# Low parts of 27 weight tiles made on GpSimd instead of VectorE, and an earlier row plan, in expert pass one of a decoder step

## What is computed

```python
q = jnp.einsum('td,dc->tc', xt, peer_wq).reshape(PEER_BLOCK, PEER_HEADS, 2, D_KEY // 2)
s = jnp.einsum('thcd,hckd->thck', q, peer_subkeys).astype(jnp.float32)
sv, si = lax.top_k(s, PEER_TOPK)
...
expert = i1 * N_KEYS + i2
gate = jax.nn.softmax(cv, axis=-1)
a = jax.nn.gelu(jnp.einsum('td,thkd->thk', xt, expert_u[expert]).astype(jnp.float32))
return jnp.einsum('thk,thkd->td', (gate * a).astype(xt.dtype), expert_v[expert])
```

## Time and profile before

| | |
|---|---|
| time, median of 3 runs | 1692.96 us (1692.66 to 1693.1) |
| profiled execution, its own time | 1686.36 us |
| its span, first to last instruction | 1684.6 us |
| TensorE, TensorE weight load | 98%, 93% busy |
| VectorE, ScalarE, GpSimd | 81%, 43%, 29% busy |
| mean granted TensorE clock | 0.994 of full |
| HBM traffic | 270 GB/s over the span |

### The profile page before, as it was taken

One profiled execution on the slowest core, in us unless ns is written; L12 is line 12 of the kernel. 1 busy time (PEld: TensorE's weight loads), 2 busy tenths in 40 slices (PEclk: granted clock), 3 DMA queues, 4 the chain that ended last, 5 costly groups with the idle time before them and its releaser, 6 DMA issues.

```text
span 1684.6 us, 29339 instructions
## 1 busy us (share of the span) xinstructions
PE 1651.6 (98%) x10256; PEld 1560.4 (93%) x10256; DVE 1368.5 (81%) x2831; ACT 732.8 (43%) x1386; POOL 489.4 (29%) x447
## 2 busy tenths in 40 slices
PE   8998999999999999999999999999999999999999
PEld 6876766679999999999999999999999999999999
DVE  3273456767889999999999989867998999999996
ACT  2121354454214434666666668833333333333332
POOL 0004222200000233322322244342443544454440
PEclk9998999999999999999999999999999999999999
DMA  7617324313225898888988899998999999999994
GB/s 221 196 38 234 92 72 120 95 52 120 75 76 173 272 336 302 285 317 302 329 321 315 312 332 356 358 377 293 355 397 358 375 402 394 399 392 398 400 386 157
DMA packets 187430, 454.16 MB, mean 270 GB/s; under 512 B 25667, under 2 KB 91715, under 8 KB 186819
## 3 DMA queue, kind: packets, MB, share of 16 engines
q1 hardware_dynamic: 110850, 242.39, 41.3%
q0 software_dynamic: 50416, 182.63, 29.5%
q10 hardware_dynamic: 26016, 27.27, 4.7%
HBM read 401.14 MB, written 54.47 MB: 270 GB/s over the span
## 4 chain that ended last, share of the span: by engine, by line
PE 62%; DVE 4%; DMA 3%; issue 1%; SPq 0%; ACT 0%; DVEq 0%; ACTq 0%
PE ps L2060 10%; PE ps L2063 10%; PE ps L2066 10%; PE ps L2036 9%; PE ps L2032 9%; PE ps L2031 9%; PE ps L2082 5%; DMA sb_ring<-expert_v 2%; DMA gates_dense<-sb_g_stage 1%; DVE sb_w_lo L1861 1%; DVE sb_slot L1898 1%; DVE sb_rows_y L1993 0%; DVE sb_hot L1897 0%; DVE sb_hot L1894 0%; DVE sb_xT_sb L2020 0%
## 5 line engine op out<-in xcount | busy, mean ns | idle before, releaser
L1766 ACT ACTIVATE sb_w_hi<-sb_ring 128x1024 fp32r<-128x1024 f32 x254 | 269.4, 1061 | 506.6 <-PE ps L2066 211.7
L1861 DVE TENSOR_TENSOR sb_w_lo<-sb_ring,sb_w_hi 128x1024 fp32r<-128x1024 f32 x255 | 312.4, 1225 | 58.8 <-ACT sb_w_hi L1766 52.4
L2031 PE MATMUL ps<-sb_x_hi,sb_w_hi 128*128 128x384 f32 x1024 | 349.7, 342 | 1.1 <-PEq L1255 1.0
L2032 PE MATMUL ps<-sb_x_lo,sb_w_hi 128*128 128x384 f32 x1024 | 345.2, 337 | 0.0
L2060 PE MATMUL ps<-sb_x_lo,sb_w_hi 128*128 128x384 f32 x1016 | 198.5, 337 | 6.2 <-ACT sb_x_lo L1775 6.1
L2036 PE MATMUL ps<-sb_x_hi,sb_w_lo 128*128 128x384 f32 x1024 | 200.8, 337 | 3.2 <-DVE sb_w_lo L1861 3.2
L2063 PE MATMUL ps<-sb_x_lo,sb_w_lo 128*128 128x384 f32 x1016 | 197.1, 336 | 0.0
L2066 PE MATMUL ps<-sb_x_lo,sb_w_hi 128*128 128x384 f32 x1016 | 196.6, 335 | 0.0
L2031 PEld LDWEIGHTS ps<-sb_x_hi,sb_w_hi 128*128 128x128 f32 x1024 | 192.0, 187 | 1.6 <-issue 1.6
L2032 PEld LDWEIGHTS ps<-sb_x_lo,sb_w_hi 128*128 128x128 f32 x1024 | 192.4, 188 | 0.0
L1756 POOL DMA_INDIRECT sb_scores<-expert_u_rows,sb_row_expert x80 | 101.0, 1263 | 293.5 <-DVE sb_row_dots L1982 206.6
(11 more groups left out here) (338 smaller groups left out, 2502.1 us busy)
## 6 DMA issues: line engine op xcount, KB each, us to landing
sb_ring<-expert_u SPq DMA_DIRECT2D x128, 512.0 KB
sb_ring<-expert_v SPq DMA_DIRECT2D x128, 512.0 KB
gates_dense<-sb_g_stage ACTq DMA_DIRECT2D x12, 2048.0 KB
hid_dense<-sb_hid SPq DMA_DIRECT2D x104, 192.0 KB
sb_scores<-hid_dense SPq DMA_DIRECT2D x104, 192.0 KB
sb_g_stage<-gates_dense SPq DMA_DIRECT2D x32, 384.0 KB
sb_g_stage<-gates_dense SPq DMA_DIRECT2D x48, 256.0 KB
sb_ring<-peer_wq SPq DMA_DIRECT2D x16, 512.0 KB
```

What stands on the lines that cost most here:

```text
L1766: nc.scalar.activation(whi[v % 2][:, :], ring(v)[:, :], ACT.Copy).then_inc(w_hi, 1)
L1861: nc.vector.tensor_tensor(wlo[v % 2][:, :], ring(v)[:, :], whi[v % 2][:, :], ALU.subtract).then_inc(w_lo, 1)
L2031: nc.tensor.matmul(out, hi[:, c * P:(c + 1) * P], g.x_hi[:, c], start=(c == 0), stop=False)
L2032: nc.tensor.matmul(out, hi[:, c * P:(c + 1) * P], g.x_lo[:, c], start=False, stop=False)
```

## The change

GpSimd gets its own `low_part(v)` for 27 units, `POOL_LO`: 2 to 6, and 14, 18, ... 98 (22 units). It waits for `w_hi` of v and the end of unit v-2, as VectorE did, and counts in a semaphore of its own, `w_lo_by_pool`; whoever waits for the low part of a unit asks `lo_of(v)` which semaphore and count that is. The five early ones stand ahead of GpSimd's first row step. Each later one stands behind row step j = `rows_done(v - 1)` + 3, a step that waits until `row_used` has reached `rows_done(v - 1)`. VectorE leaves these 27 out.

`ROW_PLAN` asks for 119 row steps by unit 101 (107 by 98 before), 149 by 116 (143), 160 by 122 (127), and starts the second half at 127 (131). The load of `quad_y` moves from SyncE's step v = 132 to 126, and the moved pieces count in its semaphore.

```diff
-ROW_PLAN = ((9, 0), (98, 107), (116, 143), (127, NR), (131, NR), (247, 2 * NR))
+ROW_PLAN = ((9, 0), (101, 119), (116, 149), (122, NR), (127, NR), (247, 2 * NR))
+FIRST_ROWS = 7
+POOL_LO = (*range(2, 7), *range(14, 102, 4))
...
+        by_pool = lambda v: sum(x < v for x in POOL_LO)
+        lo_of = lambda v: (lo_by_pool, by_pool(v) + 1) if v in POOL_LO else (w_lo, v + 1 - AHEAD_LO - by_pool(v))
...
                 if v >= NRAW + AHEAD_LO:
-                    sp.wait_ge(w_lo, v - NRAW + 1 - AHEAD_LO)
+                    sp.wait_ge(*lo_of(v - NRAW))
...
-                if v == NU + 4:
+                if v == NU - 2:
 
                     sp.wait_ge(row_used, NR)
                     sp.dma_start(quad_y[:, :], g.a["quad_h"]).then_inc(quad_in, 16)
...
         @block.gpsimd
         def _(pool):
+            def low_part(v):
+                pool.wait_ge(w_hi, v + 1 - AHEAD_U)
+                pool.wait_ge(mm, v - 1)
+                pool.tensor_tensor(wlo[v % 2][:, :], ring(v)[:, :], whi[v % 2][:, :], ALU.subtract).then_inc(lo_by_pool, 1)
+
+            for v in POOL_LO:
+                if v < FIRST_ROWS:
+                    low_part(v)
             pool.wait_ge(row_ready, 1)
             for j, (part, n) in enumerate(order):
...
+                for v in POOL_LO:
+                    if v >= FIRST_ROWS and rows_done(v - 1) + NROW - 1 == j:
+                        low_part(v)
...
             for v in range(NV):
-                if v + 1 < NV:
+                if v + 1 < NV and v + 1 not in POOL_LO:
                     prepare_weights(v + 1)
...
                 if u >= AHEAD_LO:
-                    pe.wait_ge(w_lo, u + 1 - AHEAD_LO)
+                    pe.wait_ge(*lo_of(u))
```

More of the change, by code:

```diff
@@ L1676, in experts @@
         masks, hots, g_mm, g_out = map(sem, ("masks", "hots", "g_mm", "g_out"))
-        row_ready, row_used, dots_act, quad_in, quad_moved, quad_added = map(sem, ("row_ready", "row_used", "dots_act", "quad_in", "quad_moved", "quad_added"))
+        row_ready, row_used, dots_act, quad_in, quad_added, lo_by_pool = map(sem, ("row_ready", "row_used", "dots_act", "quad_in", "quad_added", "w_lo_by_pool"))
         y_mm, y_add = map(sem, ("y_mm", "y_add"))
@@ L1732, in _ @@
                     for q in range(1, 4):
-                        sp.dma_start(moved[q - 1], quad_y[NQR * q:NQR * (q + 1), :]).then_inc(quad_moved, 16)
+                        sp.dma_start(moved[q - 1], quad_y[NQR * q:NQR * (q + 1), :]).then_inc(quad_in, 16)
                 if v == KEEP_AT:
@@ L1996, in add_quads @@
             def add_quads():
-                dve.wait_ge(quad_moved, 48)
+                dve.wait_ge(quad_in, 64)
                 for q in range(3):
@@ L2050, in v_unit @@
                 if u == NU - 1:
-                    pe.wait_ge(w_lo, v + 1 - AHEAD_LO)
+                    pe.wait_ge(*lo_of(v))
                     pe.wait_ge(c_l, u + 1)
```

## The result

The change costs 5.3%: 1781.06 us (median of 4 runs, 1773.86 to 1786.59) against 1692.81 (4 runs, 1691.67 to 1693.1) on the same chip, ratio 1.0527 [1.0500, 1.0553], or +88 us. The forecast was slower, 1750 us in 1712 to 1790: right in sign and inside the range, but the sum of +57 us was 31 too small. The profiled execution took 1781.94 us, 95.6 more than that of before.

The account below looks back on a forecast made before the run. It took TensorE as full (98% of the span), with VectorE nearly full in pass one. Terms -4 + 47 - 5 + 0 + 6 + 16 - 3 = +57 us gave 1750 us, range 1712 to 1790.

Parts of the forecast that it names:

- relief: VectorE loses 27 subtractions, 31 us of work; only TensorE's 3.2 us of pass-one waits and restarts become time: -4 us.
- waits: TensorE waits for GpSimd's low part at the 22 later units, 2.66 us minus the spare each: +47 us.
- backlog: VectorE, behind after a `look_up` at units 34, 38 and 66, catches up while TensorE stands: -5 us.
- port: GpSimd's subtractions and VectorE's two-input instructions hold each other up: +6 us, ends 0 and 25.
- clock: TensorE's granted clock drops to 0.50 behind eleven waits of 1.96 us or more, 1.45 us each: +16 us, ends 0 and 32.
- rows, ring, pass two: Earlier row steps are hidden; fewer row DMAs around the start of pass two and in it give back: -3 us (0 to -8).
- spare: Time from the end of VectorE's iteration v-1 to TensorE's first need of the low part: -4.64 us at unit 30, largest 2.7.
- faster rival: VectorE's iteration v-1 ends 3.8 us ahead of need in all 22 units, nothing late: 1681 to 1686 us, chance 0.06.
- early five: Low parts of units 2 to 6, ahead of GpSimd's first row step, are hidden by TensorE's work: 0 us.
- GpSimd's answer to the end of the iteration: Time from the last dot product of iteration v-1 until GpSimd has issued the row DMA: 1.80 us.
- the subtraction: Length of one low part on GpSimd: 2.0 us taken, between 0.95 and 3.8.
- upper bound from the four copies: Four GpSimd copies of 256 beside VectorE at 0.75 us each, so 3.0 us for a subtraction of 1024.

Follow-up runs that it names:

- plan_only: Changed kernel with no low part on GpSimd, keeping its row plan and earlier `quad_y` load: 1693.44 us, ratio 1.0019.
- early_1it: Changed kernel with each of the 22 later GpSimd subtractions one VectorE iteration earlier: 1721.86 us, ratio 1.0169.
- port_only: Changed kernel, but VectorE makes every low part and GpSimd does 22 same-size subtractions for nobody at the same places: 1721.58 us, ratio 1.0177.
- three_late: Changed kernel with only the low parts of units 30, 62 and 94 on GpSimd: 1718.15 us, ratio 1.0173.
- pick: Changed kernel with the old row plan and `quad_y` load, GpSimd only for units 2 to 6 and, two iterations earlier, 28, 31, 33: 1685.2 us.
- pick_tail: As pick, with row steps further ahead at the end of pass one and the change's earlier `quad_y` load: 1696.2 us, ratio 1.0036.
- wait_only: Changed kernel, but VectorE makes every low part and a one-column memset replaces GpSimd's 22 later subtractions, TensorE still waiting: 1743.33 us, ratio 1.0301.

## Why the prediction came out as it did

| term | predicted | measured |
|---|---|---|
| TensorE standing in pass one (relief, waits, backlog, port) | -4 + 47 - 5 + 6 = +44 | +66.5 |
| clock | +16 | +26.4 of running time, 22.3 of it under a granted clock of 0.50 |
| rows, ring, pass two | -3 | 0 |
| sum | +57 | +92.9 in the profiled pass one, +88 in the medians |

**Right: the mechanism and the places.** The subtraction went from the head of iteration v-1 to behind its end, and TensorE paid at 21 of 22 places. The single forecasts for 30, 62 and 94 were 7.3, 5.2, 4.5 us, and 7.18, 6.12, 6.71 were measured. That 7.3 and 7.18 agree is partly chance: the spare of unit 30 had grown by 2.0 us, not by 1.14, and GpSimd's answer and subtraction took 0.7 us more than assumed. Over all 22 units a single forecast missed its wait by 1.5 us in the mean; unit 14 waited 5.68 us (2.3 predicted), unit 66 0.93 (4.0). The faster rival needed each iteration to end 3.8 us ahead; only two did, those ahead of unit 70 (5.75, the one unit without a wait) and unit 98 (4.66). The early five were hidden.

**Mis-sized first: GpSimd's answer to the end of the iteration.** "The dot product ends at 1130.08, the DMA's issue at 1131.88, 1.80 us." That row was one where GpSimd stood idle. I applied it to iterations in which VectorE does two or three dot products in a row, and GpSimd still had their row DMAs to issue. The mean distance was 2.62 us, 0.82 x 22 = 18 us more. The row to look for was one with two row steps back to back on VectorE and the row DMAs behind them.

**Mis-sized second: the subtraction.** 2.0 us taken, 2.38 measured in the mean of the 22 late ones, 2.35 undisturbed; 0.38 x 22 = 8 us. The upper bound from the four copies would have been 3.0, so nothing but a choice within the bounds went wrong. Half of what the Trainium skill's page GPSIMD Engine Reference, section 3.1, gives for 2048 values was an estimate of 2.25 us. The trace comes within 0.1 us of it in the undisturbed ones, and taking it would have mended over half of this term.

**The rest of the standing time.** Both corrections make 26 us, and 22 were missing. The others are smaller, read from the two traces and in part opposed:

- The spares grew more than predicted. From the end of the last dot product of iteration v-1 to the end of TensorE's work ahead of `w_lo`, the 22 units have 11.4 us in all before and 46.3 after; the prediction had 11.4 + 22 x 1.14 + 5 for the backlog = 41.5. That is 5 us less of waits.
- The port, 6 us predicted, is no wait of its own in this account; what it did is inside the spares.
- TensorE restarts 0.05 us behind each subtraction (1 us), unit 70 has 1 us of spare more than it can use, and the relief gave 2.8 us, not 4 (1 us).
- 3.1 us are the wait for `one_hot` near the end of the pass, which the prediction had not. It stands in `plan_only` too (3.7 us) and in no kernel with another row plan. But with the plan of the change `early_1it` hasn't got it, and `port_only` and `three_late` have 0.4 and 0.5 us, so what brings it about stays open.

With these, 26 - 5 - 6 + 3 + 3 = 21 us of the 22 are accounted for.

**Port: the mechanism right, its split not shown.** The group of GpSimd's subtractions, and of VectorE's low parts in pass one of the changed kernel:

```profile
L1756 POOL TENSOR_TENSOR sb_w_lo<-sb_ring,sb_w_hi 128x1024 fp32r<-128x1024 f32 x27 | 65.0, 2409 | 66.0 <-ACT sb_w_hi L1781 65.4
```

```profile
L1876 DVE TENSOR_TENSOR sb_w_lo<-sb_ring,sb_w_hi 128x1024 fp32r<-128x1024 f32 x101 | 139.0, 1376 | 95.8 <-ACT sb_w_hi L1781 95.2 <-PEq L1255 0.3
```

The low parts there take 1376 ns, not 1.22 us. It took 31 us when VectorE had no relief (the subtraction without the wait), above my upper end of 25, and it may be a part of the 18 us that stay with the subtractions two iterations early. In the changed kernel, how much of the 66.5 us is port can't be read off. The Trainium skill's page SBUF — State Buffer, section Who interferes with whom, has whoever starts first block the other. The stretched dot product of unit 30, which began behind the subtraction and took 3.35 us, agrees. Eight VectorE instructions that began 0.05 to 0.69 us ahead of a subtraction, by the profile's starts, do not: they were held as well, and the subtraction beside them took its usual 2.35 to 2.44 us (last section).

**Mis-sized third: the clock.** I counted 11 stops at 1.45 us, the price of the first eight matmuls behind a stop. Pass one has twelve low stretches, eleven of them behind GpSimd's stops. That the number was right is partly luck: 14 stops reached the 1.96 us that I had asked for, and four of those had no low stretch behind them. And behind nine of the stops the matmuls started every 0.32 us at once, and mostly for longer than eight: 160 matmuls began under a granted clock of 0.50, 126 of them with 384 columns, and took 22.3 us longer than the same ones before, 1.9 us per low stretch. The term that was mis-sized is the price of a low stretch, taken from its first group alone. Of the other 4 us of the 26.4, 1.7 are the first matmul behind the stops at full clock, which holds the next one back (0.28 us instead of 0.17); the rest I can't place.

**Small and wrong: -3 for pass two.** It was 543 us in both kernels. Its start did gain: the first wait, which the split above counts to pass one, was 1.21 us, not 1.98, and no low stretch followed it, 1.5 us less. TensorE's later waits for ScalarE, 5.2 us in all instead of 4.1, took most of that back.

**The range.** 1712 to 1790 held the result, but not all that the prediction put into it: with the upper ends of port, clock and subtraction together its own sum gives 57 + 19 + 16 + 22 = 114 us, 1807 us.

## What to carry to other kernels

When work moves to a slack engine, write down what stands ahead of it in that engine's own queue and when that ends; here the subtraction itself was affordable and its place in a list made some four fifths of the loss. Price the answer of an in-order queue from a row where it is as loaded as it will be, not from one where it is idle. On an engine that already bounds the kernel, a stop costs its length and, behind the long ones here, a slow stretch as well, so three long stops cost nearly a third of what 21 did; the five early units and three more at places with spare on both sides were worth 0.3% together, and no more.

## What the runs showed of the hardware that I had not expected

- **A subtraction on GpSimd also held VectorE instructions that had begun before it.** VectorE instructions of 1.22 us took up to 4.15 us beside one on GpSimd. Of the 24 that were stretched in pass one, 21 ended 1.08 to 1.10 us behind the end of the subtraction, whether they had begun up to 1.9 us behind its start or up to 0.69 us ahead of it, as if they had done all their work only then. The starts on GpSimd are rough in the profile, so the order of the closest pairs is not certain. The longest, VectorE and then GpSimd of the changed kernel:

```profile
1020.14 4.15 DVE L1876 TENSOR_TENSOR sb_w_lo<-sb_ring,sb_w_hi 128x1024 fp32r<-128x1024 f32 x1 [1.14 <-ACT sb_w_hi L1781]
...
1020.83 2.37 POOL L1756 TENSOR_TENSOR sb_w_lo<-sb_ring,sb_w_hi 128x1024 fp32r<-128x1024 f32 x1
```

- **Stops of the same length end in different clocks.** Behind the stops of 2.90 us at 600.70 and 2.93 at 692.21 matmuls started every 0.32 us; behind 2.89 at 741.48 and 2.90 at 765.19 every 0.17. Stretches behind the stops of unit 42 and then unit 18 of the changed kernel (columns as in the result's stretches):

```profile
742.00:745.00 3.00, 3.00 (x25) 3.00 (x24) 2.91 (x5) 1.45 (x3) 0.00 (x0) 1.00 0.78 207
...
602.00:606.00 4.00, 4.00 (x15) 4.00 (x14) 1.19 (x2) 1.43 (x2) 1.03 (x1) 0.50 0.90 316
```

   All six stops over 4 us but none under 2.2 us was followed at once by the low level in this kernel; behind the one of 1.88 us at 834.99 the clock fell after three matmuls, at 835.6. So a stop's price is not a function of its length alone; what decides in between stays open.
- **More than one matmul rate at full clock.** In the last stretch of pass two, `pick` and `pick_tail`:

```profile
1400.00:1690.00 290.00, 280.85 (x1621) 280.52 (x1619) 251.54 (x302) 102.07 (x134) 111.00 (x81) 1.00 0.92 353
```

```profile
1400.00:1690.00 290.00, 289.23 (x1657) 288.94 (x1656) 254.76 (x303) 104.63 (x138) 106.97 (x82) 1.00 0.96 360
```

   Both show a clock of 1.00, but a matmul came every 280.85 / 1621 = 173.3 ns in one and 289.23 / 1657 = 174.5 in the other. Over all 3072 of pass two that would be 4 us. But `pick` itself ran at 174.7 in the first 800 of them, so the rate is some 3 of the 7.5 us that `pick_tail` lost there. A third rate, 176.7, held for the last 2000 matmuls of `wait_only` and for the first 800 of pass two of `early_1it`, which then ended at 173.3. What sets it I haven't found, and sums of this size carry it as an error.
